# Fused two-block model on one core: the projection products of the mixing stage in other slots of its rounds, and the gate's weights loaded with the value weights

## The reference

```
xx = token_shift(h) - h;  xr, xw, xk, xv, xa, xg = (h + xx * mu[j] for j in range(6))
r = xr @ wr;  k = xk @ wk;  v = xv @ wv
w_log = -softplus(-(w0 + tanh(xw @ w1) @ w2)) - 0.5
a = sigmoid(a0 + (xa @ a1) @ a2)
g = sigmoid(xg @ g1) @ g2
S_t = S_{t-1} diag(w_t) + (S_{t-1} a_t) b_t^T + v_t k_t^T ;  y_t = S_t r_t      (per head)
y = groupnorm(y) * ln_w + ln_b + bonus
out = (y * g) @ wo
```

## Time and profile before

| | |
|---|---|
| median of 3 runs | 3468.66 us (3462.67 to 3473.99) |
| profiled execution | 3460.95 us |
| its span | 3459.2 us |
| TensorE busy, share of the span | 3257.4 us, 94% |
| VectorE, ScalarE, GpSimd | 1644.2, 754.4, 363.0 us |
| granted TensorE clock, mean | 0.976 |

### The profile page before, as it was taken

One profiled execution on the slowest core, in us unless ns is written; L12 is line 12 of the kernel. 1 busy time (PEld: TensorE's weight loads), 2 busy tenths in 40 slices (PEclk: granted clock), 3 DMA queues, 4 the chain that ended last, 5 costly groups with the idle time before them and its releaser, 6 DMA issues.

```text
span 3459.2 us, 45630 instructions
## 1 busy us (share of the span) xinstructions
PE 3257.4 (94%) x19462; PEld 2062.2 (60%) x19462; DVE 1644.2 (48%) x3209; ACT 754.4 (22%) x1572; POOL 363.0 (10%) x282
## 2 busy tenths in 40 slices
PE   7999988999999999999998988888999999899999
PEld 3455556888884746888885444544445546434344
DVE  4565665779642226778633666564212304201011
ACT  2333331210012125211002333232222310211111
POOL 0011110222010000222000111113000001000000
PEclk9999998999999999999999999998999999899999
DMA  5322203356641320256522101000221114699997
GB/s 201 123 73 66 68 7 110 120 169 186 195 134 38 97 61 1 63 182 205 160 75 74 49 25 37 26 25 1 60 65 43 49 50 146 281 421 421 421 421 282
DMA packets 355771, 452.46 MB, mean 131 GB/s; under 512 B 25712, under 2 KB 282992, under 8 KB 331760
## 3 DMA queue, kind: packets, MB, share of 16 engines
q1 hardware_dynamic: 355568, 449.55, 38.0%
HBM read 445.27 MB, written 4.20 MB: 130 GB/s over the span
## 4 chain that ended last, share of the span: by engine, by line
PE 82%; DVE 9%; ACT 4%; DMA 4%; issue 1%; SPq 0%; POOLq 0%; POOL 0%; DVEq 0%; ACTq 0%
PE bank L79 82%; DVE A L70 2%; DMA A<-in_w_up 2%; DVE A L76 2%; ACT A L87 2%; DVE A L73 1%; PE bank L82 1%; ACT A L86 1%; DMA W<-in_w_up 1%; DVE A L2023 1%; DMA W<-in_mod_w 1%; DVE H L70 0%; ACT SM L87 0%; DVE X L76 0%; DMA A<-in_x 0%
## 5 line engine op out<-in xcount | busy, mean ns | idle before, releaser
L79 PE MATMUL bank<-A 64*64 64x64 f32 (+6 forms) x8800 | 904.3, 286 | 97.9 <-ACT A L87 49.9
L79 PEld LDWEIGHTS bank<-A 64*64 64x64 f32 (+3 forms) x8800 | 684.4, 156 | 365.2 <-issue 99.2
L79 PE MATMUL bank<-A,W 128*128 128x256 f32 (+1 forms) x2240 | 723.2, 477 | 8.5 <-DMA W<-in_rw_g 7.2
L79 PE MATMUL bank<-H,W 128*128 128x512 f32 (+2 forms) x1712 | 643.5, 526 | 23.5 <-ACT H L87 13.9
L79 PEld LDWEIGHTS bank<-A,W 128*128 128x128 f32 x2240 | 419.9, 191 | 260.8 <-issue 214.6
L87 ACT ACTIVATE A<-bank 128x512 f32<-128x512 f32 (+4 forms) x469 | 193.8, 418 | 1377.9 <-PE bank L79 1333.4
L79 PEld LDWEIGHTS bank<-H,W 128*128 128x128 f32 (+1 forms) x1712 | 317.1, 193 | 282.1 <-issue 252.2
L79 PE MATMUL bank<-A,H 128*64 128x512 f32 (+2 forms) x1224 | 309.6, 573 | 6.1 <-DMA A<-in_w_up 3.4
L70 DVE TENSOR_TENSOR A<-bank,A 128x256 f32<-128x256 f32 (+1 forms) x350 | 157.9, 462 | 177.2 <-PE bank L79 157.6
L87 ACT ACTIVATE A<-A 128x512 f32<-128x512 f32 (+1 forms) x238 | 138.2, 610 | 405.4 <-DVE A L70 367.3
L70 POOL TENSOR_TENSOR A<-A 128x512 f32<-128x512 f32 (+1 forms) x103 | 145.4, 1418 | 741.1 <-ACT A L87 381.1
(11 more groups left out here) (189 smaller groups left out, 2577.3 us busy)
## 6 DMA issues: line engine op xcount, KB each, us to landing
A<-in_w_gate SPq DMA_DIRECT2D x47, 1024.0 KB, 22.6
W<-in_mod_w SPq DMA_DIRECT2D x45, 1024.0 KB, 7.2
A<-in_w_up SPq DMA_DIRECT2D x42, 1024.0 KB, 19.2
A<-in_w_down SPq DMA_DIRECT2D x35, 1024.0 KB, 27.0
W<-in_mlp_up SPq DMA_DIRECT2D x64, 512.0 KB, 5.4
W<-in_mlp_down SPq DMA_DIRECT2D x128, 256.0 KB, 3.9
W<-in_w_mod SPq DMA_DIRECT2D x24, 1024.0 KB, 5.3
W<-in_w_up SPq DMA_DIRECT2D x22, 1024.0 KB, 19.0
```

The lines of the kernel that those rows point to most:

```text
L79: return self.e.matmul(o, l, r, start=start, stop=stop, skip_group_check=True)
```

## The change

Fetch keeps its 24 products in their order k, r, v, but a table gives each slot its number: one in slots 1, 3 and 6, two in 5, 8, 9, 11, 12, 14, 15, 17 and 22, three in 20. The waits for weights and bank stand before the first product of each eight. The k products end in slot 9, the r products in slot 15, the v products in slot 22 (before: 5, 11, 17). ScalarE's copies go to slots 10, 16 and 23. `pe_row0` of rounds 1 and 2 stays in slot 20, now behind three products. The gate's weights of blocks 0 to 3 are two further DMAs of the loads rv(4) to rv(7), in the unused half of their buffers; the gate's products of these blocks read them there, and rv is freed by the last v product as before. Blocks 4 to 7 keep loads of their own, in rounds 8 to 11. The mixing stage thus claims 36 buffers, not 40.

```
--- before.py
+++ after.py
@@ -821,22 +821,30 @@
         def fbank(ct, j):
             return (ct + j) % 2
 
+        def gate_parts(ct, off):
+            cs = slice(ct * 128, ct * 128 + 128)
+            return (off, (0, P), (128,), a["rw_g2"][0:128, cs]), (off + 128, (0, 32), (128,), a["rw_g2"][128:160, cs])
+
+        FILL = {1: 1, 3: 1, 5: 2, 6: 1, 8: 2, 9: 2, 11: 2, 12: 2, 14: 2, 15: 2, 17: 2, 20: 3, 22: 2}
+
         def sp_fetch(sp, ct):
             cs = slice(ct * 128, ct * 128 + 128)
             load(sp, ("rk", ct), (0, (0, P), (8, 128), rows128(a["rw_wk"][:, cs])), (1024, (0, P), (8, 128), rows128(a["rw_wr"][:, cs])))
-            load(sp, ("rv", ct), (0, (0, P), (8, 128), rows128(a["rw_wv"][:, cs])))
+            load(sp, ("rv", ct), (0, (0, P), (8, 128), rows128(a["rw_wv"][:, cs])), *(gate_parts(ct - 4, 1024) if ct >= 4 else ()))
 
         def pe_fetch(pe, ct, left):
 
-            yield from idle(2)
-            for j, name in enumerate(("k", "r", "v")):
-                key = ("rv", ct) if j == 2 else ("rk", ct)
-                s_, there = ring[key]
-                v = wv(s_, 1024 * (j % 2), (0, P), (8, 128))
-                b = fbank(ct, j)
-                pe.wait_ge(ring.sems[s_], there)
-                pe.wait_ge(*left[b])
-                for k in range(KT):
+            n = 0
+            for slot in range(24):
+                for n in range(n, n + FILL.get(slot, 0)):
+                    j, k = divmod(n, KT)
+                    name, key = ("k", "r", "v")[j], ("rv", ct) if j == 2 else ("rk", ct)
+                    s_, there = ring[key]
+                    v = wv(s_, 1024 * (j % 2), (0, P), (8, 128))
+                    b = fbank(ct, j)
+                    if k == 0:
+                        pe.wait_ge(ring.sems[s_], there)
+                        pe.wait_ge(*left[b])
                     pe.wait_ge(s_dv, ndv["xm", (1, 0, 2)[j], k])
                     m = pe.mm(BK[b][:, :], v[:, k, :], xm[(1, 0, 2)[j]][:, k, :], k == 0, k == 7)
                     if k == 7:
@@ -844,22 +852,21 @@
                             npe.mark_next("free", *key)
                         m.then_inc(s_pe, npe(name, ct))
                         left[b] = (s_ac, nac[name, ct])
-                    if k % 4 == 3:
-                        yield from idle(3)
-            if ct in (1, 2):
-                pe_row0(pe, ct - 1)
-            yield from idle(4)
+                n += 1 if slot in FILL else 0
+                if slot == 20 and ct in (1, 2):
+                    pe_row0(pe, ct - 1)
+                yield
 
         def ac_fetch(ac, ct):
             for j, (name, dst) in enumerate((("k", Kb2), ("r", Rb2), ("v", V2))):
-                yield from idle(6)
+                yield from idle((10, 6, 7)[j])
                 if ct >= 2:
                     ac.wait_ge(s_dv, ndv["bo", ct - 2])
                     if j == 2:
                         ac.wait_ge(s_pe, npe["tok", ct - 2, 0])
                 ac.wait_ge(s_pe, npe[name, ct])
                 ac.act(dst[ct % 2], BK[fbank(ct, j)][:, :], COPY).then_inc(s_ac, nac(name, ct))
-            yield from idle(6)
+            yield
 
 
 
@@ -1253,11 +1260,11 @@
 
 
         def sp_post(sp, ct):
-            cs = slice(ct * 128, ct * 128 + 128)
-            load(sp, ("rg", ct), (0, (0, P), (128,), a["rw_g2"][0:128, cs]), (128, (0, 32), (128,), a["rw_g2"][128:160, cs]))
+            load(sp, ("rg", ct), *gate_parts(ct, 0))
 
         def pe_post(pe, ct, left):
-            kg, tg = ring["rg", ct]
+            kg, tg = ring["rv", ct + 4] if ct < 4 else ring["rg", ct]
+            off = 1024 if ct < 4 else 0
             yield from idle(2)
             pe.wait_ge(s_ac, nac["y", ct])
             pe.wait_ge(*left[3])
@@ -1272,9 +1279,10 @@
             pe.wait_ge(ring.sems[kg], tg)
             pe.wait_ge(s_ac, nac["lo", 4])
             pe.wait_ge(*left[2])
-            pe.mm(BK[2][:, :], wv(kg, 0, (0, P), (128,)), ZG[:, 0:512], True, False)
-            npe.mark_next("free", "rg", ct)
-            pe.mm(BK[2][:, :], wv(kg, 128, (0, 32), (128,)), ZG[0:32, 512:1024], False, True).then_inc(s_pe, npe("g", ct))
+            pe.mm(BK[2][:, :], wv(kg, off, (0, P), (128,)), ZG[:, 0:512], True, False)
+            if ct >= 4:
+                npe.mark_next("free", "rg", ct)
+            pe.mm(BK[2][:, :], wv(kg, off + 128, (0, 32), (128,)), ZG[0:32, 512:1024], False, True).then_inc(s_pe, npe("g", ct))
             left[2] = (s_dv, ndv["post", ct])
             yield from idle(12)
 
@@ -1328,7 +1336,7 @@
                 if r < 8:
                     sp_fetch(sp, r)
                     sp_mod0(sp, r)
-                if r >= 4:
+                if r >= 8:
                     sp_post(sp, r - 4)
             sp.wait_ge(s_ac, nac["tok", 7, 2])
             sp.wait_ge(s_dv, ndv["bo", 7])
```

## The result

| kernel | median us (lowest to highest, runs) | ratio to the kernel before, 95% interval |
|---|---|---|
| before | 3467.47 (3461.91 to 3474.52, 10) | |
| changed | 3482.61 (3475.57 to 3486.93, 10) | 1.004 [1.0031, 1.005] |

The change costs 15 us, 0.4%. The forecast was 3472 with 3457 to 3487 around it, so the time lies inside the range, but above the likeliest case's own range (3463 to 3480) and next to rival B (3485).

The account below looks back on a forecast made before the run. TensorE, 82% of the chain of waits, was taken as the bound. Terms -7.2 - 3.8 - 10.0 + 5.6 + 7.7 + 5.0 + 4.5 = +1.8 us, plus 2 for the clock, about +4 on median 3468.66: 3472, range 3457 to 3487.

Parts of the forecast that it names:

- likeliest case: Whole kernel: the forecast itself, 3472 us, own range 3463 to 3480, chance 0.55.
- rival B: Slots 1 to 4, rounds 2 to 7: stalls over some 1.8 us lower the clock, 2.8 us each; 3485, chance 0.22.
- Gate's weights: Rounds 4 to 7: four weight waits go, -7.2 us; slow stretches in rounds 5 and 7 go, -3.8.
- Hops and groups: Rounds 3 to 7: 31 ScalarE waits filled, -10.0 us; seven more product groups a round at 0.16 each, +5.6.
- Start of a round: Slots 3 and 4, rounds 3 to 7: late md stalls TensorE 1.9 us a round; +7.7 net of old waits.
- Rounds 1 and 2: Three products fall behind round 1's bonus product and md(2) issues later: +5 us by the end of round 2.
- Round 10: Output projection: second wo load waits for rg(6)'s buffer, delaying VectorE and TensorE: +4.5 us, bounds 0 to +7.
- The clock: At the new stalls the clock may fall: 2 us added, seven stalls at 2.8 each taken for less than one.
- the clock under 1.00 in the first 10 us of rounds 3 to 7: Start of rounds 3 to 7: granted clock below full, listed as a sign that the prediction is wrong.
- slower by more: Whole kernel: slower by more than 10.4 us, most of rival B and the forecast's upper end, chance 0.25.
- no difference that could be told: Whole kernel: change within about 0.3%, 10.4 us, of the kernel before, chance 0.62.

Follow-up runs that it names:

- ring set on: Gate's weights alone with the old product slots, plus the weight-buffer ring advanced by the four saved takes, against the kernel before: 3457.47 us, 0.9968.
- two tables with fewer groups: Changed kernel with md loads ahead of rv, buffer ring advanced four takes, and products in eight groups (3461.62 us) or nine (3450.03 us).
- The early md: Changed kernel with SyncE's load order rk, md, md, rv in place of rk, rv, md, md: 3451.63 us, 0.9955 to the kernel before.
- either mend: Changed kernel with md loads ahead of rv (3451.63 us), or with VectorE's first md step in slot 4 instead of slot 1 (3457.73 us).
- table of eight groups: Changed kernel with md first, buffer ring advanced four takes, three products in each of slots 3, 6, 9, 12, 15, 18, 20, 22: 3461.62 us, 0.9977.

## Why the prediction came out as it did

- **Gate's weights: right.** -11.0 forecast. Alone it made rounds 4 to 7 13.1 us shorter; by the medians it gave 8.2 us, in spite of some 5 lost in round 10, and 11.7 with the ring set on. The slow stretches behind two waits went too, as said.
- **Hops and groups: right in sign, the groups mis-sized.** Forecast -10.0 + 5.6, so 0.9 us a round; measured 1.5 a round in the traces, 5.6 us in all by the medians. The 31 waits went. A group of two takes, from its start to the next product, about as much above its products as the 0.16 us used, but neither of the two tables with fewer groups was faster, so that price doesn't add up as assumed.
- **Start of a round: mechanism right, size too small.** The waits for SP(1) and for the masking were named with their slots. Forecast 1.9 us a round, 9.5 in five; measured 9.5 + 2.9 = 12.4. The issue of the gate parts was taken at 0.8 us and took 1.05 to 3.23.
- **Rounds 1 and 2: +5 forecast, +8.0 measured; the path right, the clock left out.** In round 1 VectorE waits 4.76 us for md, as before (4.78), so the load is no later there; three fewer products ahead of the bonus product made TensorE's wait 2.77 us, as forecast. In round 2 VectorE's first md step starts 4.6 us later (3.8 forecast). Of the 8.0 us only 3.3 are idle time of TensorE (2.1 and 1.2); 4.7 are busy time (1.8 and 2.9), at clocks of 0.94 and 0.93 where it was 1.00. What the prediction took as given, VectorE as the longer path in round 1, is itself the work of the load: with md ahead of rv and the same table the wait is gone and round 1 takes 24.4 us, less than the 25.2 of before.
- **Round 10: right.** +4.5 forecast; VectorE waited 4.07 us, TensorE 5.05, the stretch grew by 5.1.
- **The clock: this step failed.** The prediction added 2 us, "seven new stalls ... taken for less than one, since most are split in two by a product". Six of the seven stalls brought the clock to its low level, split or not; "the clock under 1.00 in the first 10 us of rounds 3 to 7" was among its own signs of being wrong, and it came in four of these five, some 10 us after the round's start. Rounds 6 and 7 against round 4 price it: 59.1 and 58.3 less 55.3, less 0.9 and 0.2 for their longer waits for SP(1) and L70, so 2.9 and 2.8 us each, as read from the kernel before. The early md took 29.7 us out of rounds 1 to 7: 15.8 of idle time, and 13.9 of busy time for the same products, which is what the clock cost. No run changed the clock alone, but the low clock stands behind each of the six stalls, and it went with them from rounds 1 and 3 to 7; round 2 keeps 0.96. Nor did a stall's length decide it as rival B had it, over some 1.8 us. By its longest piece, the stall of 1.60 and 0.60 took the clock down where 1.74 had left it; by the sum, 1.36 and 0.68 left it where 1.94 had taken it down. The Trainium skill, TensorE: Matmul & The Clock Gate, section on HAM oscillation, describes a kernel in which every burst behind a DMA wait starts slow; its waits are given as about 3 to 5 us, so it doesn't by itself say that stalls of 2 us pay, as the prediction read it. Here it was so after six stalls of seven. This had been given a rival's chance of 0.22 and was the main part of what came.

The result lies more than 10.4 us above the kernel before, the case "slower by more" that had a chance of 0.25; 0.62 went to no difference that could be told. The forecast leaned on terms of opposite sign nearly cancelling, +1.8 in sum without the clock's 2. Without the 13.9 us of clock the measured stretch grew by 0.7, so they did cancel, but in part by luck: the table gave more than forecast and the idle time of rounds 1 and 2 grew by less (3.3 against 5), while the starts of rounds and round 10 cost more (12.4 against 9.5, 5.1 against 4.5). With a sum so near zero, the size of the result was set by the term that was waved off, and the time still lies in the stated range because that reached up to 3487, past rival B's 3485.

## What to carry to other kernels

Before moving work to a later slot, ask which buffer it frees and what stands in the load queue behind that buffer's next load: here the last v product, moved by five slots, held up two loads of another stream. A wait on a load belongs as late in an in-order queue as its result allows, and loads with an early consumer ahead of those with a late one; either mend gave 25 to 31 us. Work that looks useless where it stands (four products where nothing on TensorE waits) can be the cover for another engine's late load, so read what VectorE waits for under it before thinning it, and count a stall on TensorE, such as those of 1.6 us and more here, with the slow stretch behind it (2.8 us in a round here), rather than at its own length.

## What was not expected of the hardware

- Two DMA issues of 80 KB together, each time directly behind the issue of rv, took SyncE 1.08 and 1.05 us in rounds 4 and 7 but 3.22 and 3.23 in rounds 5 and 6. Why is open.
- A wait of 1.36 us and one of 0.68 at the start of round 4 left the clock at 1.00, 1.60 and 0.60 in round 7 brought it to 0.50 for nearly 7 us.
- With the table of eight groups, the small products that need VectorE's state update started without any wait in round 4 wherever VectorE was free: the way from TensorE over VectorE and back fits under the 0.5 us of the y part there.
